# A Strassen-style FFN on TensorE: feature groups of 6, 8, 8 chunks and another order of work at the heads of the chains

## The reference

```python
def swiglu(x, w_in, w_out):
    gate, up = jnp.split(x @ w_in, 2, axis=-1)      # w_in: 1024 x 2*2816
    return (jax.nn.silu(gate) * up) @ w_out         # w_out: 2816 x 1024

x = x + 0.5 * swiglu(rms_norm(x, norm_g[l, 0]), ...)
x = x + mixer(rms_norm(x, norm_g[l, 1]))            # retention and stick-breaking, or band attention and SSD
x = x + 0.5 * swiglu(rms_norm(x, norm_g[l, 2]), ...)
```

## Time and profile before

| | us |
|---|---|
| median of 3 runs | 2066.31 (2065.22 to 2069.83) |
| the profiled execution's own time | 2062.76 |
| its span, first to last instruction | 2060.9 |
| TensorE busy | 2009.5 (98%) |
| VectorE, ScalarE, GpSimd busy | 1376.9, 1032.5, 1368.8 (67%, 50%, 66%) |

### The profile page before, as it was taken

How to read it: one execution, slowest core, us unless ns; L and a number is a source line. 1 busy time by engine, 2 the same in 40 slices (tenths; PEclk the granted TensorE clock), 3 DMA queues, 4 the chain that set the end, 5 groups by cost and what they waited for, 6 DMA issues and landing times.

```text
span 2060.9 us, 42097 instructions
## 1 busy us (share of the span) xinstructions
PE 2009.5 (98%) x16132; PEld 1960.5 (95%) x16132; DVE 1376.9 (67%) x2205; ACT 1032.5 (50%) x1983; POOL 1368.8 (66%) x1115
## 2 busy tenths in 40 slices
PE   9999999999999999999999999999999999999998
PEld 9999999999989999999999999999998799999997
DVE  7757666525757866757776685664886678567574
ACT  6646554221573655656355565542432446566561
POOL 6977865754425886875679688666643268868764
PEclk9999999999999999999999999999999999999999
DMA  4322232222112223222222222233211222222222
GB/s 159 103 84 102 90 109 97 95 104 73 67 54 83 83 92 110 101 89 98 87 83 103 88 99 102 99 116 119 88 55 39 90 103 83 103 90 99 101 93 75
DMA packets 34026, 190.86 MB, mean 93 GB/s; under 512 B 4144, under 2 KB 6704, under 8 KB 15408
## 3 DMA queue, kind: packets, MB, share of 16 engines
q1 hardware_dynamic: 26496, 173.43, 24.0%
q10 hardware_dynamic: 7344, 14.89, 2.0%
HBM read 180.81 MB, written 7.50 MB: 91 GB/s over the span
## 4 chain that ended last, share of the span: by engine, by line
PE 85%; DVE 5%; POOL 3%; ACT 3%; issue 3%; DMA 1%; POOLq 0%; ACTq 0%; SPq 0%; DVEq 0%
PE ps L787 51%; PE ps L702 15%; PE ps L717 8%; PE ps L1017 5%; POOL wl L651 1%; POOL ws L570 1%; POOL wh L647 1%; PE ps L861 1%; DMA wraw<-in_wf_in 1%; PE ps L1570 1%; PE ps L1221 1%; PE ps L1616 0%; PE ps L1596 0%; PE ps L1532 0%; DVE s L2460 0%
## 5 line engine op out<-in xcount | busy, mean ns | idle before, releaser
L787 PE MATMUL ps<-tt,ws 128*128 128x272 f32 x3840 | 524.2, 289 | 6.1 <-DVE ws L2471 6.0
L787 PEld LDWEIGHTS ps<-tt,ws 128*128 128x128 f32 x3840 | 499.1, 189 | 8.5 <-DVE ws L2471 6.9
L570 POOL TENSOR_TENSOR ws<-wraw,ws 128x512 fp32r<-128x512 f32 x312 | 403.7, 1307 | 83.4 <-ACT ws L1829 41.7
L570 POOL TENSOR_TENSOR ws<-s,ws 128x512 fp32r<-128x512 f32 x208 | 271.1, 1303 | 201.2 <-ACT ws L1867 133.1
L787 PE MATMUL ps<-u,ws 128*128 128x272 f32 x2880 | 400.9, 288 | 1.7 <-DVE tg L2521 1.0
L787 PEld LDWEIGHTS ps<-u,ws 128*128 128x128 f32 x2880 | 376.5, 188 | 2.7 <-issue 1.6
L647 POOL TENSOR_SCALAR wh<-wraw 128x1024 fp32r<-128x1024 f32 (+2 forms) x132 | 125.3, 949 | 352.8 <-PE ps L717 211.1
L651 POOL TENSOR_TENSOR wl<-wraw,wh 128x512 fp32r<-128x512 f32 (+1 forms) x255 | 345.6, 1373 | 11.0
L702 PE MATMUL ps<-u,wh 128*128 128x272 f32 x1120 | 187.6, 289 | 2.4 <-POOL wl L651 1.2
L2467 DVE TENSOR_TENSOR s<-ps,wraw 128x512 f32<-128x512 f32 x104 | 71.8, 690 | 173.6 <-POOL ws L570 173.6
L787 PE MATMUL ps<-ta,ws 128*128 128x272 f32 x1152 | 158.7, 291 | 14.7 <-DVE ws L2478 14.7
(11 more groups left out here) (411 smaller groups left out, 3939.5 us busy)
## 6 DMA issues: line engine op xcount, KB each, us to landing
wraw<-in_wf_in SPq DMA_DIRECT2D x87, 1024.0 KB, 4.8
wraw<-in_wf_out SPq DMA_DIRECT2D x32, 1024.0 KB, 4.8
wraw<-in_wf_last SPq DMA_DIRECT2D x16, 768.0 KB, 4.3
wraw<-in_w_ab SPq DMA_DIRECT2D x12, 1024.0 KB, 4.8
wraw<-in_w_cd SPq DMA_DIRECT2D x10, 1024.0 KB, 4.8
wraw<-in_w_abo SPq DMA_DIRECT2D x8, 512.0 KB, 3.2
wraw<-in_w_cdo SPq DMA_DIRECT2D x8, 512.0 KB, 3.3
wraw<-in_w_bv SPq DMA_DIRECT2D x2, 1024.0 KB, 4.8
```

Of the source, the lines that this page charges most:

```text
L570: return nc.gpsimd.tensor_tensor(wide(p, b, 1), src, wide(p, b, 0).bitcast(F32), ALU.subtract)
L787: last = nc.tensor.matmul(bank(b, 0, HT), ws[weights][w][:, i * P:(i + 1) * P], moving[:, part], start=(start and i == 0 and w == 0 and pa ...
```

## The change

Groups become 6, 8 and 8 chunks, so the output stages have K = 6, 8 and 8, and `slot`, the weight arrays and the counters follow. In `first_out`, product 1 is begun with two chunks instead of K - 3 before the last chunk of product 0. VectorE does the sums of the next chain's first period before `out_row(0)`, and ScalarE's copy of A21 for them moves to the end of the chain before. At the FFN's own head the low parts of S1 and S2 go ahead of sums 3 and 4, and the high part of S2 waits for two sums and not four. At the end of the kernel a total moves by one step.

```diff
-GROUPS = [(0, 8), (8, 16), (16, 22)]
+GROUPS = [(0, 6), (6, 14), (14, 22)]
...
         def slot(i):
-            return i % GK
+            return i - max(lo for lo, _ in GROUPS if lo <= i)
...
-                chains.append([Period(c, q + k, i, GK, (last - k) % 2, k == last, out, g)
+                chains.append([Period(c, q + k, i, GROUPS[g - 1][1] - GROUPS[g - 1][0] if out else DC, (last - k) % 2, k == last, out, g)
...
         def sums_of(f, j):
-            return 3 * (2 * GK // 2 * f + j)
+            return 3 * (GROUPS[-1][0] // 2 * f + j)
...
                 for k in range(K):
-                    if k == 4:
+                    if k == 5:
                         end_total(0)
...
-                some(1, 0, K - 3)
+                some(1, 0, 2)
                 some(0, K - 1, K).then_inc(prod_done[0], 1)
-                some(1, K - 3, K).then_inc(prod_done[1], 1)
+                some(1, 2, K).then_inc(prod_done[1], 1)
...
                 def high_s2(p, last):
-                    act.wait_ge(w_sum, 4 * p.q + 4)
+                    act.wait_ge(w_sum, 4 * p.q + (2 if g == 0 and p is p0 else 4))
...
-                a21(p0)
+                if g == 0:
+                    a21(p0)
...
                 glu_high(f, end.i)
                 if g < G - 1:
+                    a21(SEQ[f][g + 1][0])
                     act_highs(end.i // 2, 0)
                     act_highs(end.i // 2, 1)
...
                 up(1)
-                sum3(p0)
-                sum4(p0)
                 low1(p0)
                 low2(p0, True)
+                sum3(p0)
+                sum4(p0, True)
...
                     _, o0, o1, _, _ = STAGE[FFN_STAGE[f] + 2 * g + 1]
+                    sums(SEQ[f][g + 1][0])
                     out_row(0, o0 + 1)
-                    sums(SEQ[f][g + 1][0])
                     lows(SEQ[f][g + 1][0])
                     out_row(1, o1 + 1)
...
-            def sum4(p):
+            def sum4(p, behind_high=False):
                 dve.wait_ge(w_sum, 4 * p.q + 2)
+                if behind_high:
+                    dve.wait_ge(near_high, 4 * p.q + 3)
```

More of the change, by code:

```diff
@@ L374, in ffn_stages @@
         def ffn_stages(f):
-            outs_ = [ins["wf_out"][f, 0], ins["wf_out"][f, 1], ins["wf_last"][f]]
+            outs_ = [ins[f"wf_out{g}"][f] for g in range(G)]
             return [stage for g, (lo, hi) in enumerate(GROUPS) for stage in (
@@ L425, in sums_of @@
         def sums_of(f, j):
-            return 3 * (2 * GK // 2 * f + j)
+            return 3 * (GROUPS[-1][0] // 2 * f + j)
         def parts_of(f, j):
-            return 2 * (2 * GK // 2 * f + j)
+            return 2 * (GROUPS[-1][0] // 2 * f + j)
         def behind_pair(p, chunks):
@@ L539, in act_sums @@
                     pool.wait_ge(evac[0], PAIR_OF[f, 2 * j + 1] + 1)
-                k = j % (GK // 2)
+                k = slot(2 * j) // 2
                 corners = tg[:].rearrange("p b n -> p (b n)").rearrange("p (a c) -> p a c", a=2)[:, :, T:T + HT]
@@ L560, in act_low @@
             def act_low(f, j, part):
-                k, two = j % (GK // 2), slice(2 * part, 2 * part + 2)
+                k, two = slot(2 * j) // 2, slice(2 * part, 2 * part + 2)
                 pool.wait_ge(ta_high, parts_of(f, j) + part + 1)
@@ L1889, in second_row @@
                     act.wait_ge(act_ready, FC * f + p.i - 1)
-                    if p.i <= 2 * GK + 1:
+                    if p.i <= GROUPS[-1][0] + 1:
                         j = p.i // 2 - 1
@@ L3269 @@
                       for i in range(4)])
-    wf_out = np.stack([np.stack([np.concatenate([
-        pairs_of(wo[i, lo * P:hi * P], list(range(2)), GK), sevens_of(wo[i, lo * P:hi * P], list(range(2, DC)), GK)])
-        for lo, hi in GROUPS[:-1]]) for i in range(4)])
-    lo, hi = GROUPS[-1]
-    wf_last = np.stack([pairs_of(wo[i, lo * P:hi * P], list(range(DC)), hi - lo) for i in range(4)])
+    wf_out = {f"wf_out{g}": np.stack([np.concatenate([
+        pairs_of(wo[i, lo * P:hi * P], list(range(2)), hi - lo),
+        (sevens_of if g < G - 1 else pairs_of)(wo[i, lo * P:hi * P], list(range(2, DC)), hi - lo)]) for i in range(4)])
+        for g, (lo, hi) in enumerate(GROUPS)}
     ab = [4, 5, 6, 7, 20, 21, 22, 23, 0, 1, 2, 3, 8, 9, 10, 11] + list(range(12, 20))
@@ L3299 @@
         "const": const, "tab": tab, "par": par,
-        "wf_in": wf_in, "wf_out": wf_out, "wf_last": wf_last,
+        "wf_in": wf_in, **wf_out,
         "w_ab": pairs_of(f(w_in_ab)[0], ab, DC),
```

## The result

The changed kernel takes 2046.72 us (median of 4 runs, 2044.54 to 2051.10) against 2065.76 us of the kernel before on the same chip (4 runs): a ratio of 0.9908, with a 95% interval of 0.9884 to 0.9931. That is 19.0 us less; the forecast was 17.9 less. The profiled execution is the slowest of its four (2051.1, its span 2049.3), while the one of before lay under its median, so the spans differ by only 11.6 us. The changed kernel run again later had a span of 2045.2; where the two differ, both are given.

A forecast was written before the change was run, and what follows sets the result against it. The prediction took TensorE, busy for 2009.5 of 2060.9 us, as the bound, so a change pays by removing matmuls or closing holes. Its terms summed to -17.9 us, from the 2066.3 us median to 2048.4, range 2040 to 2057.

The forecast's parts named there:

- Matmuls: Over the four FFNs, 36 more matmuls on TensorE at 0.125 us each: +4.5 us.
- Heads of the third chain: Four heads behind groups of 8: the second product's 2.0 us wait goes, 0.4 at A11 stays: -8.0 us.
- Rival (b): Third chain's heads: ScalarE slips by 2.5 us, the second product waits as before, -8 is lost: 2058 us; chance 0.10.
- Heads of the second chain: Four heads behind groups of 6: 2.4 us of waits become 2.3, for A11 in GpSimd's queue: 0 us.
- Rival (a): Heads behind groups of 6 gain as well, GpSimd reaching A11 by R+9.5: -8 more, 2040 us; chance 0.08.
- FFN heads: Each FFN's first chain: low parts ahead of sums 3 and 4 start 1.2 us earlier: -4.2 us.
- Last stages and end: Last stages' first waits -5.8 us, FFN 1's two further waits -1.6, one more step at the end -0.4.
- Six-chunk output periods: Twelve periods of 63 matmuls: loads land up to 1.7 us late for the copy, +0.8 us in all.
- My sign for "wrong": The forecast would be wrong if, among other signs, 63-matmul periods started more than 8.2 us apart.
- Rival (c): Six-chunk periods: load, copy, sum 1 and evacuation set the period; at 10.5 us it costs 31: 2080 us; chance 0.06.
- Clock: TensorE's slow-clock stretches behind holes: one in place of three, -3.2 us.
- Rival (d): Change does little: holes shut, but 36 matmuls, late last chunks and port waits return most: 2064 us; chance 0.06.

The follow-up runs named there:

- experiment 2: The new order of work alone, groups kept at 8, 8, 6, against the kernel before: 2037.11 us, ratio 0.9859.
- 3: The whole change run again, unaltered, in the same set, against the kernel before: 2045.76 us, ratio 0.9902.
- experiment 11: The whole change with the first classical row's order put back as before: 2055.73 us, ratio 0.9959 to the kernel before.
- experiment 7: The whole change with A11's high and low parts ahead of the activation pair's last ones at output chains: 2039.92 us, ratio 0.9863 to the kernel before.
- experiment 5: The whole change with ScalarE's first snapshot ahead of S3's high part in an FFN's first period: 2045.18 us, ratio 0.9892 to the kernel before.
- experiment 6: The whole change with VectorE evacuating output rows ahead of sum 1 behind six-chunk output periods: 2041.78 us, ratio 0.9876 to the kernel before.
- experiment 1: The new groups 6, 8, 8 alone, order of work as before, against the kernel before: 2080.86 us, ratio 1.0071.
- experiment 10: Groups 8, 8, 6 with new order, snapshot, A11 and evacuation repairs, FFN 2's low parts one split later: 2029.48 us, ratio 0.9826 to the kernel before.
- 9: The whole change plus snapshot first, A11's parts early and evacuation first, also in the first chain's second period: 2035.84 us, ratio 0.9859 to the kernel before.

## Why the prediction was right, and where it was off

The time, the sign and the mechanism came as forecast: 2046.7 for 2048.4, within 2040 to 2057. That it came within 2 us is partly luck. The spans fell by 11.6 us in one execution of the change and by 15.7 in the other, and in the second two misses of opposite sign meet: 4.8 us too little for the six-chunk periods, 1.6 too little gain for the clock. Step by step:

- **Matmuls**: right. 16168 and not 16132; experiment 2 against 3 shows them in the cost of the groups.
- **Heads of the third chain**: right, -7.9. The second product waits no more, 0.3 us is left at A11. Rival (b), ScalarE late by 2.5 us, did not come about: the group on `ta` idles 0.0.
- **Heads of the second chain**: the reading was right, that GpSimd's activation work is the next bound there, and the number nearly: 2.3 forecast each, 1.95 measured. The sign that I gave for it, about 2 us of TensorE's wait at A11, was not: 0.70 are lost in the row and 1.25 at A11, and experiment 11 shows that one takes the place of the other. (Of GpSimd's operations there two have 272 columns and not 544; the sum doesn't hang on it.) What stretches the low part of VectorE is GpSimd's operation before it. Alone it takes 0.73 us:

```profile
335.70 0.73 DVE L2440 TENSOR_TENSOR a<-tg,a 128x544 fp32r<-128x544 f32 x1 [0.71 <-ACT a L1807]
```

In this head it took 1.60 us and ended at 87.42, 0.58 behind the end of GpSimd's L542 (85.47 + 1.37). Before, it took 1.06 and ended at 107.93, again 0.58 behind the end of GpSimd's L564 (105.99 + 1.36), and GpSimd's next operation, which began in the meantime, took 1.84 in its turn. So my reading of the earlier trace rows saw only half of it: VectorE had waited there too, 0.33 us by these times, and now waits 0.87, while GpSimd's loss goes from 0.5 us (L542) to 0.4 (L550, 1.13 us where it took 0.77 before). The Trainium skill's page "SBUF — State Buffer" (Who interferes with whom) speaks of an exclusive lock held by whichever starts first. The changed kernel's trace agrees: all 80 of these low parts that began while a GpSimd operation ran ended 0.58 or 0.59 us after it, and the other eight took 0.72 or 0.73 us.
- **Rival (a)**, that these heads gain as well, failed as it was put (operands of the queue coming earlier). Experiment 7 shows that the gain was there by another way: A11 ahead of the last activation low part.
- **FFN heads**: -4.2 forecast, -3.9 measured, by two errors that cancel. "S3's high part stays where it was" failed: it moved behind sum 3, and ScalarE's snapshot is queued behind it, 0.56 us four times. Three waits of 0.46 to 0.58 in the next period vanished, which I had not listed. Experiment 5 shows both: without the first the second comes back.
- **Last stages and end**: -7.8 forecast, -8.2 measured (9.6 to 1.7, and 0.3 at the end). With the row's order undone (experiment 11) 10.6 are lost there.
- **Six-chunk output periods**: this term was mis-sized, +0.8 for 5.8 and 5.6. The mechanism, a late load, copy, sum 1, then the evacuation, was the right one, and the "up to 1.7 us behind the copy" too small: the load at 750.46 let its copy go 6.7 us later, and I had counted on 4.8. My sign for "wrong", 63-matmul periods over 8.2 us apart, did appear. Three periods in a row have two such distances between first products, and all eight in the four FFNs are 8.23 to 10.88 us (seven of eight in the repeat). Rival (c) was the same loop at 31 us. It came at a fifth of that, and experiment 6 shows that VectorE's order behind the load sets it.
- **Clock**: -3.2 forecast. In the profiled execution it was -0.4: one slow stretch at a hole as I said, and one in the mixer, 2.8 us, which is in some executions of several of these kernels. In the repeat it was -4.8. This term is the one that single profiled executions scatter most in.
- **Rival (d)** did not come: 11.6 to 15.7 us of span.

Where I was too kind is the reading of the change as a whole. I took the groups for +4.5 of matmuls against a gain of 7.4 in the last stages. Experiments 1 and 2 show that they cost 9 to 15 us, and that the last stage's first wait, which they were to help to mend, falls to 1.1 us by the row's order alone (experiment 2, against 1.8 before), to 0.3 with both, and grows to 2.5 with the groups alone (experiment 1). The two later waits in FFN 1 (1.9 and 1.0 us) do shrink with the groups and not with the order, but experiment 10 closes them with six chunks too.

What stays open: what decides whether a hole has a slow stretch behind it (below), and why six-chunk periods wait for evacuations in the whole change and not in experiment 1. The loads are issued there at the same distance from the chain's first product (5.1 and 13.2 us in FFN 0, against 5.0 and 13.4), but TensorE, slowed by the stretch at 1.2 GHz behind the head's hole and by 0.6 us of waits, comes to the next period 7.9 us after it and not 5.7. That this delay hides the late loads is argued, not shown.

## What to carry to other kernels

Split a change into its order and its sizes and time each alone: here the order brought 29 us and the sizes gave 9 back, and the sum looked like a plain success. When a stage is shortened, look at the queue whose work does not shrink with it, and at what stands last in it: moving A11's parts ahead of the last activation parts was worth 5 to 8 us (experiment 7). In an in-order queue, put what frees a bank ahead of what waits for a load.

## What the runs showed of the hardware

- Holes of about 2 us can cost more than their length. In experiment 1 twelve places with 2.1 to 2.7 us between two starts had 3.4 us at 1.2 GHz behind them, and two more such places in the FFNs had none; before, three of the twelve heads had; in the repeat of the change, whose longest waits in the FFNs are 1.6 and 1.8, none. A hole of 2 us closed so gave up to 3.6 us back. Length alone does not decide it: experiment 11 has three holes of 2.7 us between two starts in the last stages, as experiment 1 has, and nothing behind them.
- A slow stretch of 6.8 us came up in the mixer in some executions, in code that is the same in all kernels (at 569 to 574 us in the changed kernel and in experiments 2, 7, 9 and 10; 3.4 us long in 11; in none of the others, nor before), and cost 2.8 us. One profile of each does not say what decides it.
- A load whose median from issue to landing is 4.8 us landed 6.7 us after its issue; the longest was 6.8 before, 6.5 in the repeat and 7.0 in experiment 6. There are 87 loads of this kind in the kernel, so a schedule that counts on the median meets a late one.
- A VectorE operation with two inputs in SBUF (128x544, 0.73 us alone) that starts while a GpSimd operation runs ends 0.58 us after it, whatever its start: it took 1.06 us before and 1.60 in the changed kernel for that alone. GpSimd's operation on the same shape took 1.37 us free and 1.84 when VectorE's was in its way. So most of its length in such a row is a wait.
